# Seven products of half width for 17 of the 22 gate and value pairs of an up projection

## What is computed

```
h2 = rms_norm(x, ffn_norm)
u = causal_dwconv(h2 @ w_up, conv_w, conv_b)     # w_up: 1024 x 5632, 3 taps along the tokens
a, bval = jnp.split(u, 2, axis=-1)               # 2816 gate columns, 2816 value columns
return x + (jax.nn.silu(a) * bval) @ w_down      # w_down: 2816 x 1024
```

## Time and profile before

| what | value |
|---|---|
| median of 3 runs | 1718.99 us (1718.68 to 1719.04) |
| the profiled execution | 1718.6 us, span 1716.8 us |
| mean granted TensorE clock | 0.999 |
| TensorE busy | 1704.7 us, 99% |
| VectorE, ScalarE, GpSimd busy | 1061.0, 868.3, 963.1 us |
| up stage | from 197.56 to 438.79 us of the span |

### The profile page before, as it was taken

How to read it: one execution, slowest core, us unless ns; L and a number is a source line. 1 busy time by engine, 2 the same in 40 slices (tenths; PEclk the granted TensorE clock), 3 DMA queues, 4 the chain that set the end, 5 groups by cost and what they waited for, 6 DMA issues and landing times.

```text
span 1716.8 us, 27243 instructions
## 1 busy us (share of the span) xinstructions
PE 1704.7 (99%) x9425; PEld 1440.6 (84%) x9425; DVE 1061.0 (62%) x2084; ACT 868.3 (51%) x1498; POOL 963.1 (56%) x1095
## 2 busy tenths in 40 slices
PE   9999999999999999999999999999999999999998
PEld 7778888888888778888989898977777889898988
DVE  6875755555311455568757575867776676757576
ACT  5665555555322444435545444546655554545355
POOL 5543655555555434357666666755554665656666
PEclk9999999999999999999999999999999999999999
DMA  5221333332334322223323323233322242333332
GB/s 192 74 68 61 100 98 98 97 93 93 108 95 137 104 68 83 74 74 123 99 98 99 105 96 106 64 128 116 105 97 70 87 133 91 109 99 98 99 98 74
DMA packets 48662, 167.91 MB, mean 98 GB/s; under 512 B 5376, under 2 KB 6672, under 8 KB 48528
## 3 DMA queue, kind: packets, MB, share of 16 engines
q1 hardware_dynamic: 48272, 166.05, 30.2%
q10 hardware_dynamic: 288, 0.52, 0.1%
HBM read 164.31 MB, written 2.24 MB: 97 GB/s over the span
## 4 chain that ended last, share of the span: by engine, by line
PE 90%; DVE 6%; ACT 2%; issue 1%; DMA 0%; POOL 0%; SPq 0%; DVEq 0%; ACTq 0%
PE bank L736 18%; PE bank L1444 6%; PE bank L1453 6%; PE bank L1445 6%; PE bank L661 5%; PE bank L660 5%; PE bank L666 5%; PE bank L1033 5%; PE bank L1034 5%; PE bank L1038 5%; PE bank L754 3%; PE bank L760 3%; PE bank L755 3%; PE bank L1086 2%; PE bank L1081 2%; PE bank L1080 2%
## 5 line engine op out<-in xcount | busy, mean ns | idle before, releaser
L507 POOL TENSOR_TENSOR w_lo<-stage,w_hi 128x256 fp32r<-128x256 f32 x872 | 672.2, 803 | 571.7 <-ACT w_hi L1506 317.5
L1506 ACT ACTIVATE w_hi<-stage 128x1024 fp32r<-128x1024 f32 x218 | 229.4, 1052 | 200.9 <-PE bank L1081 54.7
L660 PE MATMUL bank<-xn_hi,w_hi 128*128 128x512 f32 x544 | 211.8, 389 | 0.0
L661 PE MATMUL bank<-xn_lo,w_hi 128*128 128x512 f32 x544 | 211.7, 389 | 0.0
L736 PE MATMUL bank<-xn_hi,w_hi 128*128 128x512 f32 x464 | 189.1, 407 | 0.0
L736 PE MATMUL bank<-xn_lo,w_hi 128*128 128x512 f32 x464 | 181.8, 392 | 0.0
L2890 DVE TENSOR_TENSOR x<-x,bank 128x256 f32<-128x256 f32 (+1 forms) x217 | 97.4, 455 | 89.3 <-PE bank L1453 86.6
L1453 PE MATMUL bank<-arena 128*128 128x256 f32 x896 | 146.6, 283 | 0.0
L1033 PE MATMUL bank<-xn_hi,w_hi 128*128 128x512 f32 x352 | 137.1, 389 | 0.0
L1034 PE MATMUL bank<-xn_lo,w_hi 128*128 128x512 f32 x352 | 136.9, 389 | 0.0
L666 PE MATMUL bank<-xn_hi,w_lo 128*128 128x512 f32 x544 | 135.0, 389 | 0.0
(11 more groups left out here) (374 smaller groups left out, 3719.3 us busy)
## 6 DMA issues: line engine op xcount, KB each, us to landing
stage<-weights SPq DMA_DIRECT2D x219, 512.0 KB, 3.6
prob<-pairs SPq DMA_DIRECT2D x32, 512.0 KB, 3.6
stage<-pairs SPq DMA_DIRECT2D x32, 512.0 KB, 3.6
bias<-table SPq DMA_DIRECT2D x11, 896.0 KB, 6.4
out<-y SPq DMA_DIRECT2D x8, 256.0 KB, 2.2
x<-x_in SPq DMA_DIRECT2D x3, 512.0 KB, 7.6
bias<-swa_table SPq DMA_DIRECT2D x4, 256.0 KB, 4.4
con<-consts SPq DMA_DIRECT2D x1, 640.0 KB, 9.8
```

Source lines behind the costliest of these rows:

```text
L507: ins = nc.gpsimd.tensor_tensor(w_lo[:, p_, ks], stage[:, p_, ks], w_hi[:, p_, ks].bitcast(F32), ALU.subtract)
L660: pe.matmul(G[p_][:], w_hi[:, p_, k], hi[:, k], start=(first and k == ks[0]), stop=False)
L661: mm = pe.matmul(G[p_][:], w_hi[:, p_, k], lo[:, k], start=False, stop=False)
L1506: act.activation(w_hi[:, p_], stage[:, p_], ACT.Copy).then_inc(hi_ready, 1)
```

## The change

The first five pairs of the up projection stay as they were (`N_PLAIN`); the other 17 (`Q_UP`) are made as quads of seven products, the gate and the value tile of a pair being the two output blocks. The factors of the activation side (B11, B21, B22, T1 to T4, high and low, for 4 contraction blocks) are made once, beside the first four plain pairs: `factors(i)` on VectorE, `factor_highs(i)` on ScalarE, `factor_lows(i)` on GpSimd. For each quad ScalarE makes a copy, seven highs, and four copies of results between banks (`p1_copied`, `p5_copied`, `u2_copied`, `u3_copied`); VectorE makes four weight sums, two lows, four additions of half width (`c_00`, `c_01`, `c_1`) and the convolutions; GpSimd makes five lows and the product of gate and value (`f_made_of`), which was VectorE's. `rstd` is now in the factors, so the quads' results need no scaling. The gated blocks are no longer split along the way: `f_high` and `f_low` split them at the end of the up stage and in the first down block. Loops are written out. The weights of the 17 pairs come from the `pairs` array, 2 x 512 KB each. In the quad numbering of the second MLPs only offsets change.

```diff
-N_UP1 = 2 * NF1
+N_PLAIN = 5
+Q_UP = NF1 - N_PLAIN
+N_UP1 = 2 * N_PLAIN
...
+UP_ORDER = [HI_A11, HI_S1, HI_A12, HI_S2, HI_S4, HI_A22, HI_S3]
...
+N_IN_ARENA = 16
+POOL_LOWS = [2, 5, 8, 11, 14, 17, 20]
+DVE_LOWS = [f for f in range(NF1) if f not in POOL_LOWS]
...
+            return (G, (SUM_X, SUM_Y))[i == NF1 - 1][p_]
...
-            loads(T_MLP1 + 4, T_QKV[0])
+            def up_load(q):
+                if q == 1:
+                    sp.wait_ge(lo_ready, T_DOWN1)
+                elif q >= 2:
+                    sp.wait_ge(slot_low, UP_LOW_AT[HI_A22, q - 2])
+                if q == 2:
+                    sp.wait_ge(tile_done, T_DOWN1)
+                for r in range(2):
+                    sp.dma_start(up_raw(q, r), pairs[2 * q + r]).then_inc(quad_full[q % 2], 16)
+            loads(T_MLP1 + 4, T_MLP1 + 8)
+            up_load(0)
+            loads(T_MLP1 + 8, T_DOWN1)
+            for q in range(1, Q_UP):
+                up_load(q)
+            sp.wait_ge(slot_low, UP_LOW_AT[HI_A22, Q_UP - 1 - (Q_UP % 2)])
+            loads(T_DOWN1, T_QKV[0])
...
+            def f_made_of(i):
+                pool.wait_ge(silu_done, i + 1)
+                pool.wait_ge(conv_2, 2 * i + 2)
+                nc.gpsimd.tensor_tensor(f1[i], conv_acc(i, 0), conv_acc(i, 1), ALU.mult).then_inc(f_made, 1)
...
+            split_los(T_OUT + 6, T_MLP1 + 2)
+            for i in range(N_PLAIN - 1):
+                if i:
+                    f_made_of(i - 1)
+                split_lo(T_MLP1 // 2 + i + 1, 0)
+                factor_lows(i)
+                split_lo(T_MLP1 // 2 + i + 1, 1)
+            f_made_of(N_PLAIN - 2)
+            for k in (HI_A11, HI_A12, HI_S4):
+                up_low(k, 0)
+            for q in range(Q_UP):
+                up_low(HI_S3, q)
+                if q == 0:
+                    up_low(HI_A22, 0)
+                if q + 1 < Q_UP:
+                    up_low(HI_A11, q + 1)
+                f_made_of(N_PLAIN + q - 1)
+                if q + 1 < Q_UP:
+                    for k in (HI_A12, HI_S4, HI_A22):
+                        up_low(k, q + 1)
+            split_lo(T_DOWN1 // 2, 0)
+            split_lo(T_DOWN1 // 2, 1)
+            f_low(POOL_LOWS[0])
+            f_low(POOL_LOWS[1])
+            f_made_of(NF1 - 1)
+            for f in POOL_LOWS[2:5]:
+                f_low(f)
+            split_lo(T_DOWN1 // 2 + 1, 0)
+            for f in POOL_LOWS[5:]:
+                f_low(f)
+            split_lo(T_DOWN1 // 2 + 1, 1)
+            split_los(T_DOWN1 + 4, T_MLP2[0])
...
+            def up_product(q, k):
...
+                pe.wait_ge(slot_high, UP_HIGH_AT[k, q])
+                if k == HI_A11:
+                    if q == 0:
+                        pe.wait_ge(ffh_ready, FFH_PREP)
+                        pe.wait_ge(ff_ready, FF_PREP)
+                        pe.wait_ge(tab_sb, 2)
+                    if q < 2:
+                        pe.wait_ge(conv_2, 2 * (N_PLAIN - 2) + q + 1)
+                    else:
+                        pe.wait_ge(up_moved, moved_at(q - 2, U3_COPY))
+                elif k == HI_S1:
+                    if q == 0:
+                        pe.wait_ge(factor_low, QUADS)
+                    else:
+                        pe.wait_ge(product_added, 4 * (q - 1) + C_01)
+                elif k == HI_A12 and q:
+                    pe.wait_ge(product_added, 4 * (q - 1) + C_10)
+                elif k == HI_S2:
+                    pe.wait_ge(up_moved, moved_at(q, P1_COPY))
+                elif k == HI_S4:
+                    pe.wait_ge(up_moved, moved_at(q, P5_COPY))
+                elif k == HI_A22:
+                    pe.wait_ge(product_added, 4 * q + C_00)
+                elif k == HI_S3:
+                    pe.wait_ge(up_moved, moved_at(q, U2_COPY))
...
+            for q in range(Q_UP):
+                for k in UP_ORDER:
+                    up_product(q, k)
...
-            with act.Fori(0, NF1 // 2) as i:
-                for j in range(2):
-                    m = 2 * i + (T_MLP1 // 2 + j)
-                    for p_ in range(2):
-                        split_hi(m + 1, p_)
-                        act.wait_ge(up_scaled, 4 * i + (2 * j + p_ + 1))
...
-                        act.activation(tmp[:, 2 * j + p_], UP[2 * j + p_][:], ACT.Identity, bias=bc, scale=w2).then_inc(conv_0, 1)
-                        if p_ == 0:
-                            act.wait_ge(conv_2, 4 * i + (2 * j + 1))
-                            act.activation(UP[2 * j][:], tmp[:, 2 * j], ACT.Silu).then_inc(silu_done, 1)
-                    act.wait_ge(f_made, 2 * i + (j + 1))
-                    act.activation(f1_hi[:, bass.ds(2 * i + j, 1)].rearrange("p o s -> p (o s)"), UP[2 * j][:],
-                                   ACT.Copy).then_inc(ffh_ready, 1)
...
+            def factor_highs(k):
+                act.wait_ge(factor_made, k + 1)
+                ks = slice(k * HS, (k + 1) * HS)
+                act.activation(factor[:, F_B11, 0, ks], factor_parts[:, 0:HS], ACT.Copy).then_inc(ffh_ready, 1)
+                act.activation(factor[:, F_B21:, 0, ks], factor_parts[:, S:].rearrange("p (c s) -> p c s", c=6),
+                               ACT.Copy).then_inc(ffh_ready, 1)
...
+            def p5_copied(q):
+                act.wait_ge(product_done, N_PROD * q + UP_AT[HI_S1])
+                act.wait_ge(conv_2, 2 * (N_PLAIN + q))
...
+                act.activation(up_bank(N_PLAIN + q, 1)[:, HS:S], R5, ACT.Copy).then_inc(up_moved, 1)
...
+            for i in range(N_PLAIN - 1):
+                split_hi(T_MLP1 // 2 + i + 1, 0)
+                conv_0_of(i, 0)
+                silu(i)
+                factor_highs(i)
+                split_hi(T_MLP1 // 2 + i + 1, 1)
+                conv_0_of(i, 1)
+            act.wait_ge(tables_saved, 80)
+            up_copy(0)
+            for k in (HI_A11, HI_S1, HI_A12, HI_S2, HI_S4):
+                up_high(k, 0)
+            conv_0_of(N_PLAIN - 1, 0)
+            up_copy(1)
+            for q in range(Q_UP):
+                i, more = N_PLAIN + q, q + 1 < Q_UP
+                if q:
+                    u3_copied(q - 1)
+                silu(i - 1)
+                up_high(HI_S3, q)
+                p1_copied(q)
+                conv_0_of(i - 1, 1)
+                if q == 0:
+                    up_high(HI_A22, 0)
+                if more:
+                    up_high(HI_A11, q + 1)
+                else:
+                    split_hi(T_DOWN1 // 2, 0)
+                p5_copied(q)
+                if more:
+                    up_high(HI_S1, q + 1)
+                    up_high(HI_A12, q + 1)
+                else:
+                    split_hi(T_DOWN1 // 2, 1)
+                u2_copied(q)
+                if more:
+                    up_high(HI_S2, q + 1)
+                    up_high(HI_S4, q + 1)
+                else:
+                    f_high(0)
+                    f_high(1)
+                conv_0_of(i, 0)
+                if more:
+                    up_high(HI_A22, q + 1)
+                if q + 2 < Q_UP:
+                    up_copy(q + 2)
+            f_high(2)
+            f_high(3)
+            u3_copied(Q_UP - 1)
+            silu(NF1 - 1)
+            f_high(4)
+            conv_0_of(NF1 - 1, 1)
+            for f in range(5, 14):
+                f_high(f)
+            split_hi(T_DOWN1 // 2 + 1, 0)
+            for f in range(14, NF1):
+                f_high(f)
...
+            def factors(k):
...
+                if k:
+                    dve.wait_ge(ffh_ready, 2 * k)
+                    dve.wait_ge(ff_ready, 2 * k)
+                    dve.wait_ge(factor_low, k)
+                b11, b12, b21, b22 = [e[:, c * HS:(c + 1) * HS] for c in range(4)]
+                t1, t3, t2, t4 = [e[:, c * HS:(c + 1) * HS] for c in range(4, 8)]
+                dve.scalar_tensor_tensor(out=e[:, 0:S], in0=x[:, k], scalar=pcol("ffn_norm", k, k + 1), in1=rstd[:],
+                                         op0=ALU.mult, op1=ALU.mult)
+                dlink(dve.scalar_tensor_tensor(out=e[:, S:2 * S], in0=x[:, k + 4], scalar=pcol("ffn_norm", k + 4, k + 5), in1=rstd[:],
+                                               op0=ALU.mult, op1=ALU.mult))
+                dve.tensor_tensor(t1, b12, b11, ALU.subtract)
+                dlink(dve.tensor_tensor(t3, b22, b12, ALU.subtract))
+                dlink(dve.tensor_tensor(t2, b22, t1, ALU.subtract))
+                dve.tensor_tensor(t4, b21, t2, ALU.subtract).then_inc(factor_made, 1)
+                ks = slice(k * HS, (k + 1) * HS)
+                dve.wait_ge(ffh_ready, 2 * k + 1)
+                dve.tensor_tensor(factor[:, F_B11, 1, ks], b11, factor[:, F_B11, 0, ks].bitcast(F32), ALU.subtract).then_inc(ff_ready, 1)
+                dve.wait_ge(ffh_ready, 2 * k + 2)
+                dve.tensor_tensor(factor[:, F_B21:F_T1, 1, ks], e[:, S:2 * S].rearrange("p (c s) -> p c s", c=2),
+                                  factor[:, F_B21:F_T1, 0, ks].bitcast(F32), ALU.subtract).then_inc(ff_ready, 1)
...
```

(53 more changed lines are left out.)

338 lines of the change are left out of this document (245 added, 93 removed).

## The result

| | before | after |
|---|---|---|
| median of the runs, us | 1718.7 | 1727.5 |
| ratio | | 1.005, 95% interval 1.0036 to 1.0065 |
| profiled execution and its span, us | 1718.6, 1716.8 | 1727.9, 1725.5 |
| mean granted clock | 0.999 | 0.997 |

A forecast was written before the change was run, and what follows sets the result against it. TensorE's matmuls were taken to bound the kernel, busy 99% of the span. The terms, -13.6 + 9.6 + 0 + 4.6 = +0.6 us on a profiled 1718.6, gave 1719.2, as a median 1719.6; range 1711.5 to 1729.5.

The forecast's parts named there:

- The gain, 13.6 us: Up stage on TensorE: seven products take 10.08 us a pair instead of 10.88, so 17 pairs gain 13.6 us.
- two prices of a gap: Time from one matmul to the next: measured rows 120 and 227 ns, the skill's formula 109 and 216; the rows decide.
- The stage of products costs nothing: The 17 pairs of products: other engines keep TensorE's pace, 0 us lost; upper bound 5 us.
- Plain pairs, +7.0: Plain pairs: VectorE's chain with the factors takes 11.9, then 13.0 us, over TensorE's 10.88; TensorE is 7.0 us late.
- Into the products, +2.6: Way from the plain pairs into the first quad: products wait for VectorE's and ScalarE's work; lag grows from 7.0 to 9.6.
- Into the down phase, +4.6 with bounds 3.5 and 5.5: Start of the down phase: TensorE waits for lows made behind the last product; 4.6 us lost, bounds 3.5 and 5.5.
- the low of f 3, and f 4, 6, 7 by E + 8.0: Start of the down phase: VectorE finishes these lows 8.0 us after the last product ends (E).
- The ring: Slower rival, product stage: VectorE and ScalarE need 10.4 us a pair, over 10.08; 5 us more, 1724.6; chance 0.18.
- that rival: TensorE's waits drop its clock to 1.2 GHz, each tile then at half speed costing 5.44 us more: 1725; chance 0.03.
- Dear plain pairs and tail: Slower rival: high prices in the plain pairs (+3 us) and the start of the down phase (+1); chance 0.15.
- no change: Whole kernel: the forecast, 1719.6 us, can't be told from before, within about 0.2% or 3.4 us; chance 0.44.
- the likeliest case: Whole kernel: the forecast's own case, 1716 to 1722.5 us, without the rivals.

The follow-up runs named there:

- the last run: The changed kernel with factor inputs read from banks, all lows on VectorE and the down phase's begin reordered: 1712.3 us, ratio to before 0.9962.

## Why the prediction was right and wrong

- **The gain, 13.6 us.** Right. Quads are 10.08 us apart to the hundredth, and of the two prices of a gap the row's was the one to take. The Trainium skill (TensorE: Matmul & The Clock Gate, "Back-to-back issue gap") gives the formula that the prediction quotes for a matmul by itself, not for a kernel's stream of weight loads and matmuls.
- **The stage of products costs nothing.** Right, with its ring of VectorE and ScalarE; the hand-overs of written out code hold. A reason I hadn't given adds to it: all of VectorE's operations there read a bank, and the last run showed such operations unblocked.
- **Plain pairs, +7.0, measured +9.2.** The mechanism was right (VectorE's chain is longer than 10.88, felt through ScalarE's and GpSimd's splits; TensorE's waits are for `w_hi` at 1.26 and for `w_lo` at 0.89). The first pair was 11.56 for 11.9. The step that failed is the price beside GpSimd: 4.2 us for the six operations and 13.0 for the pair; they took 5.2 (220.89 to 226.07), and the pair 13.6, since the low that I priced at 0.95 took 0.69. A slip in the sum is a part of it: 1.05 + 1.18 + 0.5 + 0.58 + 0.9 has five terms for six operations; with a sixth, of 0.45 to 0.9, it is 4.7 to 5.1. Three of the subtractions (0.84, 0.95, 0.85; the fourth 0.43) and the two wide ones (0.94, 1.22) each wait for an operation of GpSimd's, and GpSimd waits for them: `factor_lows` took 2.90, above my bounds of 2.4 to 2.7, and the split of the gate tile 4.10 for 2.83. I had taken GpSimd's rows as fixed.
- **Into the products, +2.6, measured +2.0.** Right within its size: S2 for `p1`'s copy, S4 for `p5`'s.
- **Into the down phase, +4.6 with bounds 3.5 and 5.5, measured +10.9.** The step that failed is "the low of f 3, and f 4, 6, 7 by E + 8.0" at 0.7 to 0.96 each, and "then waits no more". VectorE's lows of f 3, 4, 6 and 7 took 5.9 us together, 1.7 each for three of them, with GpSimd's product and lows beside them, the first tile got through 8.9 late instead of 5.0, and a second wait, 1.71 for GpSimd's low of f 17, came behind a split and another low. I took 0.96, the dear price of a 256 wide operation, for a 512 wide one, though the earlier trace rows has 1.23 for a 512 wide row, and none of these prices holds beside a longer operation of GpSimd's. The upper bound was no bound.
- **Rivals.** The ring didn't come. The clock fell in the down phase, as that rival said with a chance of 0.03, but without its price of 5.44 us a tile: it cost nothing that can be told, since the lows were later at any clock. Dear plain pairs and tail came, with a chance of 0.15 as against 0.44 for no change, at +8 instead of the +4 that I gave them: 2.2 for the 3 of the plain pairs, 6.3 for the 1 of the tail. Two terms rested on the same price with the same doubt; they were bound to miss together, and the range of the likeliest case, 1716 to 1722.5, treated them as small and separate. That the time lies in the whole range is luck: its upper end was made of the ring's 5 us, which didn't come, and without them it would have been about 1724.5, below the 1727.5 measured.

## What to carry over

Before work is split between VectorE and GpSimd, ask of each VectorE operation whether both inputs are in SBUF. If so, and GpSimd reads SBUF, the two take turns by whole instructions: add the instruction of the one to the price of the other, and a 512 wide low given to GpSimd holds a low of VectorE's up by about 1.1 where they meet (1.75 for 0.69), and saves it 0.6. Let VectorE's operation read one input from a bank, or put GpSimd's work beside such operations. An idle half of an engine is no room as long as its neighbour holds the way to the memory. And where one unmeasured price stands in several terms of a sum, move them together when the range is made.
